# Layer boundaries by token tile in a two-block float32 kernel: 128-column matmuls for the first two weight units of each wide layer

## The reference, cut to what matters

```python
x = x + gla_mixer(rmsnorm(x, norm_mix[0]), ...)          # "mix0", output projection "GO"
x = x + conv_ffn(rmsnorm(x, norm_ffn[0]), ...)           # "ffn0": h @ w_up, 3-tap conv, silu(gate)*val, @ w_down
x = x + attn_mixer(rmsnorm(x, norm_mix[1]), ...)         # "mix1": kv, q, attention, "AO"
x = x + conv_ffn(rmsnorm(x, norm_ffn[1]), ...)           # "ffn1"
x = x + recurrent_mixer(rmsnorm_2(x, norm_g[0]), ...)    # "lru"
x = x + shortconv_mixer(rmsnorm_2(x, norm_g[1]), ...)    # "sc"
return rmsnorm_2(x, final_g)
```

## Time and profile before

| | |
|---|---|
| median of three runs | 942.03 us (941.36 to 942.67) |
| profiled execution, first to last instruction | 941.0 us |
| mean granted TensorE clock | 0.976 |
| PE busy, PEld busy | 888.9 us (94%), 811.1 us (86%) |
| DVE, ACT, POOL busy | 621.8, 499.8, 35.1 us |
| DMA read and written | 150.88 and 1.05 MB, 161 GB/s |

### The profile page before, as it was taken

One profiled execution on the slowest core, in us unless ns is written; L12 is line 12 of the kernel. 1 busy time (PEld: TensorE's weight loads), 2 busy tenths in 40 slices (PEclk: granted clock), 3 DMA queues, 4 the chain that ended last, 5 costly groups with the idle time before them and its releaser, 6 DMA issues.

```text
span 941.0 us, 15040 instructions
## 1 busy us (share of the span) xinstructions
PE 888.9 (94%) x5816; PEld 811.1 (86%) x5816; DVE 621.8 (66%) x814; ACT 499.8 (53%) x647; POOL 35.1 (4%) x77
## 2 busy tenths in 40 slices
PE   5999798999999989798999999989999899999996
PEld 5988678999999968577999999979999789999995
DVE  5498655776766767775777676657886566645643
ACT  6366344655545453364554554538988664443431
POOL 2000100000000021201000000000000000000001
PEclk9999988999999999799999999999999989999998
DMA  8443441464553515134546445435355036445421
GB/s 324 147 173 135 178 167 61 176 228 174 195 207 137 220 51 218 45 108 184 182 177 222 179 167 211 157 134 200 115 201 202 1 135 224 161 176 220 157 88 45
DMA packets 22340, 152.43 MB, mean 162 GB/s; under 512 B 2496, under 2 KB 2624, under 8 KB 5024
## 3 DMA queue, kind: packets, MB, share of 16 engines
q1 hardware_dynamic: 21936, 149.45, 43.1%
q0 software_dynamic: 368, 2.49, 0.7%
HBM read 150.88 MB, written 1.05 MB: 161 GB/s over the span
## 4 chain that ended last, share of the span: by engine, by line
PE 87%; DVE 5%; ACT 5%; issue 1%; POOL 1%; DMA 0%; POOLq 0%; ACTq 0%; DVEq 0%
PE ring L1185 52%; PE acc L1198 27%; PE acc L1346 2%; PE ring L1334 1%; PE ring L1428 1%; ACT h_hi L437 1%; ACT xn L428 1%; PE ring L1382 1%; PE acc L1406 1%; PE ring L1167 1%; DVE h_lo L730 1%; DVE w_lo L714 0%; DVE xn L721 0%; DVE x L744 0%; PE ring L1243 0%
## 5 line engine op out<-in xcount | busy, mean ns | idle before, releaser
L1185 PE MATMUL ring<-h_hi,w_hi 128*128 128x256 f32 x1344 | 385.0, 286 | 6.2 <-DVE h_lo L730 4.0
L714 DVE TENSOR_TENSOR w_lo<-raw,w_hi 128x2048 fp32r<-128x2048 f32 (+1 forms) x146 | 317.8, 2200 | 108.5 <-ACT w_hi L419 108.2
L1185 PE MATMUL ring<-h_lo,w_hi 128*128 128x256 f32 x1344 | 383.3, 285 | 0.0
L1185 PE MATMUL ring<-h_hi,w_lo 128*128 128x256 f32 x1344 | 383.3, 285 | 0.0
L419 ACT ACTIVATE w_hi<-raw 128x2048 fp32r<-128x2048 f32 (+1 forms) x146 | 264.2, 1840 | 23.5 <-DMA raw<-in_stream_dram 15.0
L1185 PEld LDWEIGHTS ring<-h_hi,w_hi 128*128 128x128 f32 x1344 | 259.3, 193 | 9.1 <-issue 5.2
L1185 PEld LDWEIGHTS ring<-h_lo,w_hi 128*128 128x128 f32 x1344 | 259.3, 193 | 1.7
L1185 PEld LDWEIGHTS ring<-h_hi,w_lo 128*128 128x128 f32 x1344 | 259.2, 193 | 0.0
L899 DVE SCALAR_TENSOR_TENSOR cacc<-ring,par,cacc 128x255 f32<-128x255 f32 x176 | 76.9, 478 | 58.0 <-ACT cacc L521 53.0
L1198 PE MATMUL acc<-w_hi,a_hi 128*128 128x512 f32 x272 | 107.0, 393 | 3.9 <-DVE a_lo L1085 2.6
L1198 PE MATMUL acc<-w_hi,a_lo 128*128 128x512 f32 x272 | 107.0, 393 | 0.0
(11 more groups left out here) (195 smaller groups left out, 768.9 us busy)
## 6 DMA issues: line engine op xcount, KB each, us to landing
raw<-in_stream_dram SPq DMA_DIRECT2D x134, 1024.0 KB, 4.8
raw<-in_stream_dram SPq DMA_DIRECT2D x12, 512.0 KB, 5.3
gatew<-in_gatew_dram POOLq DMA_DIRECT2D x1, 1536.0 KB, 6.7
x<-in_x_dram SPq DMA_DIRECT2D x2, 512.0 KB, 3.8
out_dram<-xn SPq DMA_DIRECT2D x2, 512.0 KB, 2.6
row<-in_row_dram POOLq DMA_DIRECT2D x1, 640.0 KB, 8.9
par<-in_par_dram SPq DMA_DIRECT2D x1, 274.0 KB, 4.8
rope<-in_rope_dram POOLq DMA_DIRECT2D x1, 256.0 KB, 9.2
```

The costliest lines, as they stand in the source:

```text
L714: nc.vector.tensor_tensor(w_lo[:, u % RING, 0:n], raw[:, u % RAW, 0:n], w_hi[:, u % RING, 0:n].bitcast(f32), ALU.subtract).then_inc(lo_spl ...
L1185: last = nc.tensor.matmul(ring[:, b, f * S:(f + 1) * S], w_parts[a][:, slot, lo:lo + P], h_parts[c][:, kc, :], start=kc == 0 and n == 0, s ...
```

## The change

1. **`first_pair`** replaces the first two wide units of ffn0, ffn1, lru and sc. Both units are done for token tile 0 (96 matmuls with 128 moving columns), then both for tile 1 (96 more). Chunk by chunk for tile 0, unit by unit for tile 1. The transposes of tile 1 are issued in the middle of tile 0's matmuls.
2. **The boundary by tile.** Transposes go to `acc` instead of `ring`. DVE multiplies by the norm's weight (`xn` again, two instructions of 128x512 a tile), ACT copies to `h_hi` (two), DVE subtracts to `h_lo` (two). `boundary` sets the order: DVE does `normed(0)` ahead of the last residual half, ACT the last sum behind tile 0's copies. At mix0, turn and ffn0 the order is written out around `split` calls.
3. **Orders on PE.** The GO projection runs tile by tile, with the transposes of "turn" tile 1 and of ffn0 tile 0 inside it; kv runs tile by tile; the rank product uses two halves of 128 moving columns (weights of 32 columns).
4. **No clearing.** `clear_acc`, its operand `zeros` and its memset go; the first tall unit (`(e, i) == (0, 0)`) starts the accumulation, taken out of the loop.
5. **Moves.** The lambda table goes behind `split(3)`, ahead of the evictions of q and k. The second unit of sc (`U_SC + 1`) is split at the end of lru. `sg` lies in another buffer.

```diff
+            def turned(name, t):                                   # DVE
+                for b in range(2):
+                    c = C_GAMMA[name] + 4 * b
+                    dve.wait_ge(x_turned, HALVES[name] + 2 * t + b + 1)
+                    nc.vector.tensor_tensor(by_kc(xn[:, t, b * 512:(b + 1) * 512]), by_kc(acc[:, t, b * 512:(b + 1) * 512]),
+                                            par[:, c:c + 4].unsqueeze(2).to_broadcast([P, 4, P]), ALU.mult).then_inc(h_full_ready, 1)
+                for b in range(2):
+                    ...
+                    nc.vector.tensor_tensor(h_lo[:, 4 * b:4 * b + 4, t * P:(t + 1) * P], by_kc(xn[:, t, b * 512:(b + 1) * 512]),
+                                            part.bitcast(f32), ALU.subtract).then_inc(h_lo_ready, 1)
+            def boundary(layer, units, name):                      # DVE
+                residual(layer, units, 0)
+                residual(layer, units, 1, (0,))
+                normed(name, 0)
+                residual(layer, units, 1, (1,))
+                turned(name, 0)
+                normed(name, 1)
+                turned(name, 1)
+            def boundary(name):                                    # ACT
+                sums(0, name)
+                sums(1, name, (0,))
+                turned(name, 0)
+                sums(1, name, (1,))
+                turned(name, 1)
+            def turn(name, t):                                     # PE
+                pe.wait_ge(xn_ready, XN[name] + t + 1)
+                for kc in range(KC):
+                    last = nc.tensor.transpose(acc[:, t, kc * P:(kc + 1) * P], xn[:, t, kc * P:(kc + 1) * P], ident[:, :])
+                    if kc % 4 == 3:
+                        last.then_inc(x_turned, 1)
+            def first_pair(name, u0, banks, turned_first=False):
+                if not turned_first:
+                    turn(name, 0)
+                for u in (u0, u0 + 1):
+                    ready(u)
+                for kc in range(KC):
+                    h_half(name, 0, kc)
+                    if kc == 4:
+                        turn(name, 1)
+                    for k, b in enumerate(banks):
+                        for f in range(2):
+                            for n, (a, c) in enumerate(PARTS):
+                                lo = kc * 256 + f * P
+                                nc.tensor.matmul(ring[:, b, f * S:f * S + P], w_parts[a][:, (u0 + k) % RING, lo:lo + P],
+                                                 h_parts[c][:, kc, 0:P], start=kc == 0 and f == 0 and n == 0,
+                                                 stop=kc == KC - 1 and n == 2, skip_group_check=True)
+                for k, b in enumerate(banks):
+                    for f in range(2):
+                        for kc in range(KC):
+                            if k == 0 and f == 0:
+                                h_half(name, 1, kc)
+                            for n, (a, c) in enumerate(PARTS):
+                                lo = kc * 256 + f * P
+                                last = nc.tensor.matmul(ring[:, b, f * S + P:(f + 1) * S], w_parts[a][:, (u0 + k) % RING, lo:lo + P],
+                                                        h_parts[c][:, kc, P:S], start=False,
+                                                        stop=kc == KC - 1 and n == 2, skip_group_check=True)
+                    last.then_inc(used, 1)
-                up(0)
-                pe.wait_ge(acc_free[0], FREED[f"ffn{n}"])
-                pe.wait_ge(acc_free[1], FREED[f"ffn{n}"])
-                clear_acc()
+                first_pair(f"ffn{n}", B, (G % 4, (G + 1) % 4), turned_first=n == 0)
+                up(1)
+                down(0, B + 4)
-            turn("gla", GEN["norm_turn"])
+            turn("turn", 0)
+            for t in range(T):
+                for n in range(4):
+                    if (t, n) == (0, 2):
+                        turn("turn", 1)
+                    if (t, n) == (1, 3):
+                        turn("ffn0", 0)
+                    h_half("turn", t, 2 * n)
+                    tall(U_GO + n, of_h, (2 * n, 2 * n + 1), first=n == 0, end=n == 3, layer_ends=n == 3, tiles=(t,))
+            for t in range(T):                                     # DVE, "turn" and ffn0
+                turned("turn", t)
+            split(16)
+            split(17)
+            residual(1, U_GO + 4, 0)
+            normed("ffn0", 0)
+            split(18)
+            turned("ffn0", 0)
+            split(19)
+            residual(1, U_GO + 4, 1)
+            normed("ffn0", 1)
+            turned("ffn0", 1)
```

More of the change, by code:

```diff
@@ L107 @@
 LRU_UNIT = lru_plan()
[L109 removed]
+BRANCH_BANK, GATE_BANK, *HEAD_BANKS = ((GEN["lru"] + n) % 4 for n in range(4))
 SCORE_BANKS = [GEN["qT"] % 4, (GEN["qT"] + 1) % 4]
@@ L419, in split, with sums @@
                 nc.scalar.activation(w_hi[:, u % RING, 0:n], raw[:, u % RAW, 0:n], ACT.Copy).then_inc(hi_split, 1)
-            def sums(t, name):
-                for half in range(2):
+            def sums(t, name, halves=(0, 1)):
+                for half in halves:
                     if name != "mix0":
@@ L544, in ffn @@
                 step(FFN_ITERS - 1, last=True)
[L546 to L550, removed]
+            sums(0, "ffn0")
+            split(18)
+            turned("ffn0", 0)
+            split(19)
+            sums(1, "ffn0")
+            turned("ffn0", 1)
             split(20)
             ffn(0)
-            for t in range(T):
-                sums(t, "mix1")
-            turned("mix1")
+            boundary("mix1")
             for u in range(U_KV + 3, U_KV + 6):
@@ L598, in _ @@
                 split(u)
-            for t in range(T):
-                sums(t, "ffn1")
-            turned("ffn1")
+            boundary("ffn1")
             split(U_FFN[1] + 4)
             ffn(1)
-            for t in range(T):
-                sums(t, "lru")
-            turned("lru")
+            boundary("lru")
             split(U_LRU + 3)
@@ L664, in _ @@
                     split(u)
[L667 to L670, removed]
+            boundary("sc")
+            for u in range(U_SC + 2, U_SC + 4):
                 split(u)
@@ L735, in residual, with normed @@
[L735 to L745, removed]
+            def normed(name, t):
+                dve.wait_ge(rms_ready, RMS[name] + t + 1)
+                nc.vector.tensor_scalar(xn[:, t, :], x[:, t, :], rstd[:, t:t + 1], None, ALU.mult).then_inc(xn_ready, 1)
@@ new lines, in residual @@
+            def residual(layer, units, t, halves=(0, 1)):
+                for half in halves:
+                    if (t, half) != (T - 1, 1):
+                        dve.wait_ge(bank_done, (2 * T - 1) * (layer - 1) + 2 * t + half + 1)
+                    else:
+                        dve.wait_ge(used, units)
+                    at = slice(half * 512, (half + 1) * 512)
+                    nc.vector.tensor_tensor(x[:, t, at], acc[:, t, at], x[:, t, at], ALU.add).then_inc(
+                        (half_added, acc_free[t])[half], 1)
@@ L1088, in _ @@
                     split(u)
-            residual(5, U_SC)
-            normed("sc")
-            turned("sc")
-            for u in range(U_SC + 1, U_SC + 4):
+            boundary(5, U_SC, "sc")
+            for u in range(U_SC + 2, U_SC + 4):
                 split(u)
@@ L1135, in _ @@
             sc_step(SC_ITERS - 1, splits=0)
-            residual(6, UNITS)
+            for t in range(T):
+                residual(6, UNITS, t)
             dve.wait_ge(rows_loaded, 32)
```

283 lines of the change are left out of this document (125 added, 158 removed).

## The result

The changed kernel takes 1019.29 us (median of four runs, 1007.09 to 1035.20) against 941.69 for the one before on the same chip: ratio 1.0756 [1.0704, 1.0807]. This ratio goes by the fast runs alone, of which the change has two (1007.09 and 1016.18 us), while the medians stand 8.2% apart. The forecast was 968, range 944 to 988: the sign was right and the size missed by 51 us. The four runs differ in one thing that the records show: at 1007.09, 1016.18, 1022.41 and 1035.20 us the mean granted clock was 0.949, 0.941, 0.933 and 0.921. Half of the added low-clock time accounts for these distances (0.949 to 0.921 is 2 x 0.028 x 1020 = 57 us more at the lower level, 29 us lost, against 28 measured).

What follows compares the result with a forecast made beforehand. PE was taken as the bound, holding 87% of the chain of waits. ffn1 +5.8, sc +5.3, lru +8.1, kv -1.4, ffn0 +2.6, start +2.3, clock +3 sum to +25.7 on 941.0: 966.7, told as 968 us, range 944 to 988.

Steps and rivals of the forecast that it cites:

- Pace of a narrow matmul, 0.110 us: First pairs of four layers: each matmul of 128 moving columns takes 0.110 us, set by its weight load; +9.6 a layer.
- rival 1: Moving columns alone set the pace, 0.066 us a matmul: 33.8 us come off, 934 us; chance 0.07.
- rival 2: Weight loads overlap in part: pace 0.088 us, 951 us in all (944 at 0.079); chance 0.04.
- rival 4: fp32r with a narrow moving operand runs like plain float32, 0.216 us a matmul: 1049 us; chance 0.06.
- First wide matmul at E + 3.5, tile 1 hidden, transposes 0.9: Boundaries, from E (start of last residual addition): first wide matmul 3.5 us later, tile 1's preparation hidden, its transposes 0.9 us.
- The start, +2.3: Kernel start: first wide matmul at 19.5 instead of 17.19, behind tile 1's added DVE work; +2.3 us that stays.
- GO: GO projection, with the lambda table moved: can start at about 118.0 instead of 120.37 and ends at 143.5.
- The stall in ffn0's tile 0: ffn0's first pair: PE waits 1.5 us for tile 1 after 48 matmuls; the pair ends at 167.1 against 164.50, +2.6.
- The table under q and k: Lambda table's new place costs nothing if q and k (24.78 us of PE) cover it; otherwise up to 4.9 us.
- kv, -1.4: kv boundary, tile by tile without a pair: done 15.4 us after E against 16.8, a gain of 1.4 us.
- The clock, +3: Falls to 1.2 GHz in the first pairs: two of 1.5 us each assumed, +3 us; bounds 0 and 79 us.
- Rival 3: The clock stays at 1.2 GHz through all first pairs: 79 us in place of 3, 1044 us; chance 0.06.

Runs made afterwards that it cites:

- experiment 3: Kernel before, with only the second pair of units of ffn0, ffn1 and sc, amid steady work, at 128 moving columns: 972.19 us, ratio 1.0326.
- (5): Changed kernel plus unread 512-column matmuls in PE's waits at the boundaries of ffn0, ffn1, lru and sc: 971.40 us, ratio 1.0328.
- (6): Kernel before with the first pair of each wide layer narrow, plus unread 512-column matmuls in PE's waits at five boundaries: 978.13 us, ratio 1.0405.
- Experiment 1: Changed kernel with the first pairs back at 256 moving columns, started when both tiles are ready, the rest kept: 963.52 us, ratio 1.023.
- experiment 2: Kernel before, with only the first pair of units of ffn0, ffn1, lru and sc at 128 moving columns: 1062.88 us, ratio 1.127.
- experiment 4: Changed kernel with tile 1's pass of each first pair at 256 moving columns, computing tile 0 again: 1008.86 us, ratio 1.0678.
- the kernel of 934.94 us: Kernel before with the lambda table moved, no clearing and unread 512-column matmuls in PE's waits at five boundaries: 934.94 us, ratio 0.9944.

## Why the prediction missed

- *Pace of a narrow matmul, 0.110 us.* Right: 0.111 in experiment 3 and 0.112 in tile 1's pass. The weight loads bind (0.06 with 32-column weights), +9.9 us a pair for the forecast 9.6. The Trainium skill, "TensorE: Matmul & The Clock Gate", section Back-to-back issue gap, has about 81 ns for this width; here no stretch at full clock with 128-column weights comes below 0.110. Rivals 1, 2 and 4 fall by that. The argument against rival 1, that two loads never overlap, isn't what the rows show: each load lasts 0.19 and starts 0.11 behind the last. It is the distance of the starts that held.
- *First wide matmul at E + 3.5, tile 1 hidden, transposes 0.9.* Right: 3.7 at ffn1, 3.6 at lru, 3.5 at kv. At sc 4.3, since `split(U_SC + 1)`, which was taken as hidden, holds DVE to 801.46 and with it the residual additions: 0.8 us. E to the steady step, forecast as 25.6, is 32.7, 32.4 and 32.9; less the 6.9 us that a fall of 13.7 us costs it is 25.8, 25.5 and 26.0.
- *The start, +2.3.* Measured +3.1 at the first wide matmul, as tile 1's half of the rank product ran at the lower level, and +2.4 at z. *GO:* started at 119.32; forecast were 118.0 and the start's delay, 120.4, so 1.1 us had been made up on the way: before, the clock was low from 45.3 to 48.7 in z's products, and now it wasn't. *The stall in ffn0's tile 0,* 1.5 us: from 151.02 to 152.57, right in length, but the clock fell in it. The table under q and k cost nothing.
- *kv, -1.4.* Wrong by 2.5: +2.5 to the q rotation, of which the attention gave 1.4 back (its falls lasted 3.4 us, before 10.2). Already kv's last matmul ends at E + 17.0, not 15.4, as its first 12 ran at the lower level (timeline):
```profile
380.08 0.39 PE L1373 MATMUL ring<-w_hi,h_lo 128*128 128x512 f32 x1
```
  The sum had no fall here. It also stopped at kv's last matmul and didn't follow the weight splits behind tile 1's `h`, where 2.3 us more were lost.
- *The clock, +3.* This is the step that failed. It measured +38: three falls of 13.7 us at 6.9 each, and in ffn0 17.7 (20.3 less the forecast 2.6; half of the 37.5 us at the lower level is 18.8, and 1.1 had been made up ahead of GO). With it in place of the 3, and 2.5 for kv, the sum is 968 - 3 + 38 + 2.5 = 1005.5, against 1007.09. The median has another 12 us, by more low-clock time. Two falls of 1.5 us had been taken from the pair of before, where 256 columns brought the clock back within the pair. Nothing spoke for that with 128 columns; the prediction had named the half-empty array and then priced it with the full one's number. Rival 3 named the mechanism, and gave it 0.06 and the extreme of all pairs low. The truth lay at half of it (38 of 79), a case that neither the likeliest nor the range held, since the range reached only to one low pair. Its reason was also off: the narrow stream doesn't pull the clock down (experiment 3); without the waits filled it falls, with them filled it doesn't ((5) and (6)), and the stream keeps it where it is. With the falls filled away the rest of the sum stands: 968 - 3 + 2.5 = 967.5, and (5) takes 971.40.
- The boundary that the change was to shorten got its first matmul 2 us earlier and paid 10 us of pace for it. Experiment 1 shows the other arm: at full width the tile order would have to be paid with the wait for both tiles, +2.3%.

## What to carry to other kernels

A matmul with a fresh 128-column weight has a floor of 0.11 us here, so splitting the moving operand into halves to start sooner nearly doubles its cost (0.111 each against 0.120 for both). Splitting along the contraction gave 0.5 us a boundary where both weights were there, filling the waits more. Price the clock by what runs behind a wait, not by what ran there before: with 256 columns a fall at a boundary lasted 3 to 10 us, with 128 it lasted 14 to 48. When one part is moved ahead on PE, follow what its queue mates on ScalarE and VectorE free, down to the transfer that waits for the buffer.

## What was unexpected of the hardware

- A stream that keeps PE at 39.20 of 39.20 us busy stays at 1.2 GHz, and the same stream stays at 2.4 GHz if it starts there. The Trainium skill, "Perfetto Trace Analysis", section Matmul Optimizations, asks that matmuls execute back-to-back in batches for the engine's power scaling; here 192 back-to-back in a batch weren't enough in experiment 2, and the 256-column ones behind them were.
- The falls had the same length in ffn1, lru and sc of the change, 13.7 us, with eight transposes of 128 columns in their middle, and 41 to 48 us in experiment 2 without them; but ffn0's lasted 37.5 with them, and lru's and sc's in experiment 4 outlasted them too (20.5 and 23.9). What ends a fall within a narrow stream stays open.
- Unread matmuls are worth their place: 13 a boundary, 65 in all, belong to the kernel of 934.94 us; the change with 36 of them, and with its kv order mended, takes 969.84, still 3.2% above before.
